# A hybrid decoder block on eight cores: the first tiles' weights by GpSimd's casting DMA, the norm weights in the row scaling, and some bf16 copies stored one tile later

## The chip, the cores and the metric

The kernel runs on all eight cores of one Trainium2 chip. Each core computes one element of the batch (8192 rows of 1024) and nothing is exchanged between cores. The metric is device time in microseconds of the slowest core.

## The reference, cut to what matters

```python
h   = rms_norm(x, norm1_g)               # y * g, y = x * rsqrt(mean(x*x) + eps)
cols = h @ w_in                          # 4864 columns: q f i g | q k v | gate_a gate_b
o_a = hgrn2_branch(...)                  # gated linear recurrence
o_b = swa_sink_attention(...)            # sliding window 128, 8 heads on 2
mixed = sigmoid(gate_a) * (o_a @ w_branch_a) + sigmoid(gate_b) * (o_b @ w_branch_b)
x   = x + mixed @ w_out
h2  = rms_norm(x, norm2_g)
x   = x + conv_glu(h2, w_up, conv_w, conv_b, w_down)   # width 2816, conv of 3 on the gate half
```

All inputs are float32. The norm weight `g` multiplies the columns of `h`, which are the rows of `w_in` (and of `w_up`), so it can be put into either factor.

## The kernel before

A core works through 16 tiles of 512 rows. For each tile `stage_a` (here A(0) to A(15)) computes everything up to `x + mixed @ w_out` and stores that as `x1scr`; `stage_f` (F(0) to F(15)) reads it back and computes the gated MLP. Inside a tile four blocks of 128 rows are normalised by `norm_block` (sum of squares on ScalarE, a power on GpSimd, the row scaling on VectorE into `xs`, transposes on TensorE, copies into `hT` or `h2T`).

The weights are cut into 61 pieces of 128 x 2048: 27 of kind A (numbers 0 to 26: f, q, aq, akv, i, g, eight gab, four wab, four wo) and 34 of kind F (22 up, 12 dn, four of the dn only 128 x 1536). They don't fit in SBUF, so every tile loads every piece again. `load_piece` does this. In tiles 1 to 15 it is one DMA on SyncE's queue, bf16, from the scratch tensor `wscr` into one of five slots `wA` or five slots `wF`. In tile 0 the source is the float32 tensor `wall`: two DMAs bring the halves of a piece into staging buffers (five in the memory of `act` for kind A, four `stg` for kind F), VectorE and ScalarE in turn multiply 128 x 256 blocks by the norm weight into the slot (or copy, for the unscaled wab, wo and dn), and the slot is then stored to `wscr`.

The order of the work on each engine is written by a planner (`schedule`): it simulates all operations with costs (`DMA_GBPS` 280, 450 ns for an issue on SyncE) and puts each engine's operations into a queue in the order of their simulated start. The chip keeps that order; every operation waits on semaphores for what it depends on. Priorities let F(i) run beside A(i+1). The chains `alA` and `alF` keep the pieces in order.

Of the kernel before, what the change touches and what calls it, by code (L numbers as in the profile page):

```python
# [9 lines left out]
F32 = mybir.dt.float32  # L10
BF16 = mybir.dt.bfloat16
# [4 lines left out]
D = 1024  # L16
# [12 lines left out]
CAPS = dict(pA=6, pF=5)  # L29
TUNE = dict(rF=1, skew=4, gc=0, foff=0.2, hold=6000.0)  # L30

# [11 lines left out]
class Pool:  # L43
    def __init__(self, name, aps):
        self.name = name
        self.aps = aps
        self.free = [(0.0, i) for i in range(len(aps))]
        self.last = [[] for _ in aps]
        self.sem = [None] * len(aps)
        self.used = {}  # L50

# [89 lines left out]
class Prog:  # L141
# [177 lines left out]
    def finalize(self):  # L319
        for e in ENGS:  # L320
            for o in self.q[e]:
                if o.dsem is not None:
                    s = o.dsem
                    if isinstance(s, VBuf):
                        if s.pool.sem[s.slot] is None:
                            s.pool.sem[s.slot] = self.new_sem()
                        s = s.pool.sem[s.slot]
                        o.dsem = s
        for o in sorted((o for o in self.ops if o.dsem is not None), key=lambda o: (o.start, o.idx)):
            self.sem_counts[o.dsem] += 16  # L330
            o.dval = self.sem_counts[o.dsem]
        for e in ENGS:
            for o in self.q[e]:
                for p in o.deps:
                    if p.dsem is None and self.needs(p, o):
                        p.signals = True
        for e in ENGS:
            c = 0
            for o in self.q[e]:
                if o.signals:  # L340
                    c += 1
                    o.sigval = c
# [158 lines left out]
def build_program(seq=SEQ):  # L501
    ntile = seq // T
    nc = bass.Bass("TRN2", target_bir_lowering=False, dynamic_dma_scratch_size=1024)
    dt_in = lambda name, shape, dt=F32: nc.dram_tensor(name, list(shape), dt, kind="ExternalInput").ap()
# [5 lines left out]
    cb_d = dt_in("cb", [128, CBN], BF16)  # L510
    c_mask = dt_in("c_mask_st", [128, 128])
    c_dm = dt_in("c_dm", [128, 2, 2, 4, 128], BF16)
    y_d = nc.dram_tensor("y", [seq, D], F32, kind="ExternalOutput").ap()
# [4 lines left out]
    with ExitStack() as es:  # L518
# [14 lines left out]
        mask_st = sb("mask_st", [128, 128], F32)  # L533
        dm = sb("dm", [128, 2, 2, 512], BF16)

# [38 lines left out]

        pWA = mkpool("wA", 5, [2048], BF16)
        pWF = mkpool("wF", 5, [2048], BF16)
        pST = mkpool("stg", 4, [1024], F32)
        pXT = mkpool("xt", 4, [D], F32)
        pX1 = mkpool("x1", 4, [D], F32)
        pSA = P.pool("sa", [act[:, 4 * i_:4 * i_ + 4, :].rearrange("p a n -> p (a n)").bitcast(F32) for i_ in range(5)])  # L580
        pXS = mkpool("xs", 2, [D], BF16)
        pFA = mkpool("fa", 8, [T], F32)
# [80 lines left out]
        def DMA(out, in_, reads, writes, sem, nbytes, eng="sp", slow=False, chain=None):  # L663
            def fn(h):
                if slow:
                    return h.dma_start(out=res(out), in_=res(in_), allow_slow_non_contiguous=True)
                return h.dma_start(out=res(out), in_=res(in_))  # L667
            return P.record(eng, fn, reads, writes, 450.0 if eng == "sp" else 100.0, 2000.0, SET_ANY, sem, nbytes, chain)

# [25 lines left out]
        cload("cf", cft[:], cf_d, 126976)  # L695
        cload("cbb", cbt[:], cb_d, 294912)
        cload("mask", mask_st[:], c_mask, 65536)
        cload("dm", dm[:], c_dm.rearrange("p a b g t -> p a b (g t)"), 524288)
# [48 lines left out]
        pidx = {(p["kind"], p["name"]): i for i, p in enumerate(pieces)}  # L747
        first_f = {}
        last_ld = {}
        bx1 = {}  # L750
# [3 lines left out]
        def load_piece(ti, kind, name):  # L754
# [6 lines left out]
            size = nk * cols  # L761
            if ti > 0:
                P.link("al" + kind, DMA(w[:, 0:size], wscr[i, :, 0:size], [bwscr[i]], [w], w, size * 256))
                return w
            hs = size // 2
            for hv in range(2):
                st = vb(pSA if kind == "A" else pST, f"st{name}{hv}")
                o_ = DMA(st[:, 0:hs], wall[i, :, hv * hs:(hv + 1) * hs], [], [st], st, hs * 512, chain="ld" + kind)
                first_f.setdefault(kind, o_)
                last_ld[kind] = o_  # L770
                if kind == "F" and first_f["F"] is o_:
                    after(o_, last_ld["A"])
                nh = nk // 2
                if p["scale"] is None:
                    eng = "dve" if hv == 0 else "act"
                    o_ = CP(eng, w[:, hv * hs:(hv + 1) * hs], st[:, 0:hs], [st], [w], n=hs, rate=2.0)
                    if hv == 0:
                        P.link("al" + kind, o_)
                else:
                    g = g1 if p["scale"] == "g1" else g2  # L780
                    koff = name[1] * 4 if name[0] == "i" else 0
                    for kk in range(nh):
                        kc = hv * nh + kk
                        o_ap, i_ap = w[:, kc * cols:(kc + 1) * cols], st[:, kk * cols:(kk + 1) * cols]
                        sc = g[:, koff + kc:koff + kc + 1]
                        if kk % 2 == 0:
                            o_ = TS("dve", o_ap, i_ap, sc, None, ALU.mult, None, [st] + C("cf"), [w], n=cols, rate=1.5)
                            if kc == 0:
                                P.link("al" + kind, o_)
                        else:  # L790
                            A(o_ap, i_ap, AF.Copy, [st] + C("cf"), [w], n=cols, scale=sc, nap=1)
                if kind == "A":
                    for o2 in st.users:
                        for c_ in range(NFC):
                            bact[c_].r.append(o2)
            if ntile > 1:
                DMA(wscr[i, :, 0:size], w[:, 0:size], [w], [bwscr[i]], P.new_sem() if False else w, size * 256)
# [5 lines left out]
        def norm_block(which, b, xv, hdst, bhdst, pool):  # L803
# [18 lines left out]
        def stage_a(ti):  # L822
# [285 lines left out]
def _in_maps(inputs, seq, n_cores):  # L1108
# [23 lines left out]
    shared["c_mask_st"] = consts["mask_st"]  # L1132
    shared["c_dm"] = consts["dm"]
    maps = []
    for c in range(n_cores):
# [12 lines left out]
```

How the kernel before makes its waits and increments, by code:

```python
    def emit(self, eng, h, ws, esems, dsems):  # L396
        for o in self.q[eng]:
            for key, val in ws[o]:
                h.wait_ge(esems[key[1]] if key[0] == "e" else dsems[key[1]], val)
            inst = o.fn(h)
            if o.dsem is not None:
                inst.then_inc(dsems[o.dsem], 16)
            elif o.signals:
                inst.then_inc(esems[eng], 1)
```

## Time and profile before

| | |
|---|---|
| times of three runs | 3827.41, 4324.09, 3821.53 us; median 3827.41 |
| profiled execution | 3824.09 us, its span 3822.6 us |
| spans of the eight cores | 3808.2 to 3822.6 us |
| granted TensorE clock, mean | 0.984 to 0.988 |
| busy | TensorE 95%, ScalarE 58%, VectorE 53%, GpSimd 12% |
| moved by the DMA engines | 772.82 MB, mean 202 GB/s |

The profile is of the slowest core. "Busy" is time in which an engine had an instruction in work. A window row gives, for one stretch, the busy time of each engine with its number of instructions, the granted TensorE clock as a share of full speed, the mean busy share of the core's 16 DMA engines and what they moved.

### The profile page before, as it was taken

To read this page: it belongs to the slowest core of one execution; us is meant where nothing else is said; L and a number is where in the kernel's file an instruction comes from. 1 tells how busy PE (TensorE), PEld (TensorE's weight loads), DVE (VectorE), ACT (ScalarE), POOL (GpSimd) and SP (SyncE) were. 2 spreads that over 40 slices of the span, in tenths; PEclk is the share of its full clock that TensorE was granted. 3 is DMA by queue.
4 is the path that set the end of the run, shared out by engine and by line. 5 is a ranking of instruction groups with operands and counts; after the bars stand their busy time and mean duration, and the time that the engine had idled before them with its cause. 6 is when DMAs were issued, how large, how long until landed. Compare 5 with 4: busy or idle time off the path is not lost.

```text
span 3822.6 us, 65864 instructions; the slowest of 8 cores (3808.2 to 3822.6 us)
## 1 busy us (share of the span) xinstructions
PE 3648.7 (95%) x21516; PEld 1969.4 (52%) x21516; DVE 2041.4 (53%) x3455; ACT 2204.0 (58%) x3771; POOL 448.0 (12%) x1082
## 2 busy tenths in 40 slices
PE   5778989999999999999999999999999999999989
PEld 2334454645546464554645546464554646455455
DVE  4546645455564546556464555645556464555634
ACT  6859566374664737467473755737466472746622
POOL 0100101101020110101011010110102011010100
PEclk8889999999999999999999999999999999999999
DMA  8798975646557465664746556474655746566454
GB/s 252 225 293 237 270 255 168 230 159 233 187 174 234 160 211 181 207 207 161 248 155 212 182 191 227 156 237 150 233 185 179 237 158 213 173 214 200 149 201 147
DMA packets 214317, 772.82 MB, mean 202 GB/s; under 512 B 23776, under 2 KB 24160, under 8 KB 213984
## 3 DMA queue, kind: packets, MB, share of 16 engines
q1 hardware_dynamic: 213408, 767.65, 60.5%
q8 instruction: 182, 2.98, 0.3%
q14 instruction: 151, 1.24, 0.1%
q10 hardware_dynamic: 576, 0.95, 0.1%
HBM read 669.94 MB, written 98.57 MB: 201 GB/s over the span
## 4 chain that ended last, share of the span: by engine, by line
PE 85%; ACT 6%; DMA 4%; issue 3%; DVE 1%; SPq 1%; POOL 0%; ACTq 0%; DVEq 0%; POOLq 0%
PE bank L651 85%; DMA wF<-wscr 3%; ACT fa L607 2%; DMA stg<-wall 1%; ACT ef L607 1%; ACT L607 1%; DMA wA<-wscr 1%; SPq L667 1%; ACT ba L607 0%; DVE fa L629 0%; ACT wF L607 0%; ACT wA L607 0%; PE bank L659 0%; ACT hT L607 0%; ACT xs L608 0%
## 5 line engine op out<-in xcount | busy, mean ns | idle before, releaser
L651 PE MATMUL bank<-h2T,wF 128*128 128x512 bf16 x5632 | 1290.5, 380 | 41.2 <-ACT ef L607 25.3
L651 PE MATMUL bank<-hT,wA 128*128 128x512 bf16 x4224 | 997.0, 387 | 48.5 <-ACT wA L607 21.3
L651 PEld LDWEIGHTS bank<-h2T,wF 128*128 128x128 bf16 x5632 | 536.5, 98 | 703.9 <-issue 97.2
L651 PEld LDWEIGHTS bank<-hT,wA 128*128 128x128 bf16 x4224 | 413.4, 99 | 527.9 <-issue 91.4
L624 DVE SCALAR_TENSOR_TENSOR ef<-bank,cft,ef 128x512 f32<-128x512 f32 x704 | 520.1, 747 | 281.9 <-ACT ef L607 236.6
L651 PE MATMUL bank<-wF,act 128*128 128x256 bf16 x5632 | 653.3, 273 | 8.7 <-DMA wF<-wscr 8.7
L651 PEld LDWEIGHTS bank<-wF,act 128*128 128x128 bf16 x5632 | 546.8, 98 | 109.4 <-issue 11.0
L607 ACT ACTIVATE ef<-bank,cft 128x512 f32<-128x512 f32 x352 | 273.2, 776 | 430.1 <-PE bank L651 383.0
L629 DVE TENSOR_TENSOR act<-ef,bank 128x512 bf16<-128x512 f32 x352 | 241.3, 686 | 406.5 <-PE bank L651 402.1
L607 ACT ACTIVATE hT<-bank 128x512 bf16<-128x512 f32 x128 | 74.3, 595 | 437.6 <-PE bank L651 436.9
L607 ACT ACTIVATE fa<-fa 128x512 f32<-128x512 f32 x400 | 239.4, 629 | 111.4 <-DVE gsum L629 105.0
L607 ACT ACTIVATE ef<-ef 128x512 f32<-128x512 f32 x352 | 213.9, 626 | 153.3 <-DVE ef L624 151.4
L607 ACT ACT_TABLE_LOAD x231 | 296.4, 1283 | 10.2 <-DVE og L619 6.1
L629 DVE TENSOR_TENSOR x<-bank,x 128x256 f32<-128x256 f32 x256 | 107.0, 422 | 284.0 <-PE bank L651 283.9
L651 PE MATMUL bank<-wA,mixT 128*128 128x512 bf16 x1024 | 234.6, 381 | 1.4 <-POOL mixT L629 1.4
L607 ACT ACTIVATE fa<-bank,sinkexp 64x128 f32<-64x128 f32 x512 | 185.3, 362 | 51.7 <-PE bank L651 24.1
L629 POOL TENSOR_TENSOR nst<-nst,mhalf 128x1 f32<-128x1 f32 x128 | 71.3, 558 | 1209.5 <-DVE nst L619 1207.4
L629 DVE TENSOR_TENSOR fa<-bank,dm 128x512 f32<-128x512 f32 x254 | 165.5, 683 | 33.8 <-PE bank L651 33.1
L607 ACT ACTIVATE ba<-fa,negshift 128x512 bf16<-128x512 f32 x254 | 171.2, 713 | 3.8 <-DVE fa L629 1.8
L624 DVE SCALAR_TENSOR_TENSOR xt<-bank,xt 128x512 f32<-128x512 f32 x128 | 88.0, 690 | 159.1 <-PE bank L651 151.2
L635 POOL COPY halo<-ef 128x2 f32<-128x2 f32 x352 | 73.8, 210 | 806.7 <-DVE ef L624 806.0
L629 POOL TENSOR_TENSOR mixT<-mixT,gbuf 128x512 bf16<-128x512 bf16 x128 | 149.5, 1169 | 136.3 <-DVE gbuf L624 135.9
(93 smaller groups left out, 3419.3 us busy)
## 6 DMA issues: line engine op xcount, KB each, us to landing
wF<-wscr SPq DMA_DIRECT2D x450, 512.0 KB, 4.5
wA<-wscr SPq DMA_DIRECT2D x405, 512.0 KB, 4.6
xt<-x SPq DMA_DIRECT2D x128, 512.0 KB, 6.1
x1scr<-xt SPq DMA_DIRECT2D x64, 512.0 KB, 4.1
xt<-x1scr SPq DMA_DIRECT2D x64, 512.0 KB, 6.9
x<-x1scr SPq DMA_DIRECT2D x64, 512.0 KB, 9.8
y<-x SPq DMA_DIRECT2D x64, 512.0 KB, 5.5
stg<-wall SPq DMA_DIRECT2D x60, 512.0 KB, 11.1
```

The costliest lines, as they stand in the source:

```text
L607: return h.activation(out=res(out), in_=res(in_), func=func, scale=scale, bias=bias)
L624: return P.record("dve", lambda h: h.scalar_tensor_tensor(out=res(out), in0=res(in0), scalar=scalar, in1=res(in1), op0=op0, op1=op1), read ...
L629: return P.record(eng, lambda h: h.tensor_tensor(out=res(out), in0=res(in0), in1=res(in1), op=op), reads, writes, cost)
L635: return P.record(eng, lambda h: h.tensor_copy(out=res(out), in_=res(in_)), reads, writes, cost)
L651: inst = h.matmul(res(out), lhsT=res(lhsT), rhs=res(rhs), start=st, stop=sp_)
L667: return h.dma_start(out=res(out), in_=res(in_))
```

## The change

In `load_piece`, a piece's first load is one DMA from `wall` (float32) issued by GpSimd, which casts to bf16 on the way straight into the slot. No staging buffers and no multiplications by VectorE or ScalarE are left. The norm weights come as a constant `c_g`, repeated over 128 partitions, and are loaded into `gB0` and `gB1`; `norm_block`'s row scaling is a scalar_tensor_tensor that multiplies by the row's factor and by `gB`. A list `keep_at` says in which tile a piece's bf16 copy is stored to `wscr`: tile 0 for pieces 0 to 17 of kind A and 0 to 9 of kind F, tile 1 for the last 9 of kind A (one gab, four wab, four wo) and the last 24 of kind F (12 up, 12 dn). These 33 pieces are loaded from `wall` by GpSimd in tile 0 and once more in tile 1. The slots of `xs` go from two to four, and a slot has a semaphore of its own for GpSimd's loads. The planner is told 1000 ns for an issue on GpSimd.

```diff
-TUNE = dict(rF=1, skew=4, gc=0, foff=0.2, hold=6000.0)
+TUNE = dict(nxt=4, nxs=4, nwa=5, nwf=5, dA=18, dF=10, dF2=99, rF=1, skew=4, gc=0, foff=0.2, hold=6000.0)
...
-    nc = bass.Bass("TRN2", target_bir_lowering=False, dynamic_dma_scratch_size=1024)
+    nc = bass.Bass("TRN2", target_bir_lowering=False, dynamic_dma_scratch_size=4096)
...
-        pST = mkpool("stg", 4, [1024], F32)
...
-        pSA = P.pool("sa", [act[:, 4 * i_:4 * i_ + 4, :].rearrange("p a n -> p (a n)").bitcast(F32) for i_ in range(5)])
-        pXS = mkpool("xs", 2, [D], BF16)
+        pXS = mkpool("xs", int(TUNE["nxs"]), [D], BF16)
...
+        cload("gB0", gB[0][:], c_g[0], 524288)
+        cload("gB1", gB[1][:], c_g[1], 524288)
...
+        keep_at = [(1 if i >= TUNE["dA"] else 0) if p["kind"] == "A" else (2 if i - na >= TUNE["dF2"] else 1 if i - na >= TUNE["dF"] else 0) for i, p in enumerate(pieces)]
...
-            if ti > 0:
+            at = keep_at[i]
+            if ti > at:
                 P.link("al" + kind, DMA(w[:, 0:size], wscr[i, :, 0:size], [bwscr[i]], [w], w, size * 256))
                 return w
-            hs = size // 2
-            for hv in range(2):
-                st = vb(pSA if kind == "A" else pST, f"st{name}{hv}")
-                o_ = DMA(st[:, 0:hs], wall[i, :, hv * hs:(hv + 1) * hs], [], [st], st, hs * 512, chain="ld" + kind)
...
+            o_ = DMA(w[:, 0:size], wall[i, :, 0:size], [], [w], w, size * 512, eng="pool")
+            P.link("al" + kind, o_)
+            last_ld[kind] = o_
+            if kind not in first_f:
+                first_f[kind] = o_
+                if kind == "F":
                     after(o_, last_ld["A"])
...
-                    for kk in range(nh):
-                        kc = hv * nh + kk
-                        o_ap, i_ap = w[:, kc * cols:(kc + 1) * cols], st[:, kk * cols:(kk + 1) * cols]
-                        sc = g[:, koff + kc:koff + kc + 1]
-                        if kk % 2 == 0:
-                            o_ = TS("dve", o_ap, i_ap, sc, None, ALU.mult, None, [st] + C("cf"), [w], n=cols, rate=1.5)
-                            if kc == 0:
-                                P.link("al" + kind, o_)
-                        else:
-                            A(o_ap, i_ap, AF.Copy, [st] + C("cf"), [w], n=cols, scale=sc, nap=1)
...
-            if ntile > 1:
+            if ti == at and ntile > at + 1:
                 DMA(wscr[i, :, 0:size], w[:, 0:size], [w], [bwscr[i]], P.new_sem() if False else w, size * 256)
             return w
...
-            TS("dve", xs.lz(), xv.lz(), st4[:, b, 2:3], None, ALU.mult, None, [xv, bn], [xs], n=D, rate=1.6)
+            STT(xs.lz(), xv.lz(), st4[:, b, 2:3], gB[which][:], ALU.mult, ALU.mult, [xv, bn] + C(f"gB{which}"), [xs], n=D, psum=False)
...
-                after(o_, P.chain["ldA" if ti == 0 else "alA"])
+                after(o_, P.chain["alA"])
```

## Rows read from the trace of the kernel before

**Rows 1.** The page: the span, and TensorE and its clock in 40 slices of 95.6 us
```profile
span 3822.6 us, 65864 instructions; the slowest of 8 cores (3808.2 to 3822.6 us)
...
PE   5778989999999999999999999999999999999989
...
PEclk8889999999999999999999999999999999999999
```

**Rows 2.** Timeline of SyncE's queue: start, us, the issues of y stores
```profile
561.79 1.27 SPq L667 DMA_DIRECT2D y<-x  x1
...
758.77 0.59 SPq L667 DMA_DIRECT2D y<-x  x1
...
984.95 0.40 SPq L667 DMA_DIRECT2D y<-x  x1
...
1211.66 0.62 SPq L667 DMA_DIRECT2D y<-x  x1
...
3478.68 0.72 SPq L667 DMA_DIRECT2D y<-x  x1
```

**Rows 3.** Windows: length, PE, PEld, DVE, ACT, POOL, PEclk, DMA share, GB/s
```profile
0.00:206.00 206.00, 137.31 (x637) 61.11 (x637) 103.46 (x215) 142.16 (x259) 23.80 (x39) 0.86 0.80 244
206.00:449.00 243.00, 200.77 (x993) 89.95 (x993) 146.06 (x279) 176.08 (x316) 27.46 (x67) 0.94 0.85 260
449.00:562.00 113.00, 97.91 (x679) 62.81 (x680) 46.66 (x88) 67.14 (x109) 4.54 (x8) 0.95 0.82 262
562.00:759.00 197.00, 188.81 (x1111) 102.88 (x1109) 105.00 (x171) 97.62 (x159) 24.82 (x61) 1.00 0.61 202
...
985.00:1212.00 227.00, 224.87 (x1347) 122.42 (x1346) 123.32 (x205) 131.49 (x225) 27.78 (x67) 1.00 0.59 196
```

**Rows 4.** Windows of 20 us, the same columns; nine had a DMA share from 0.98
```profile
140.00:160.00 20.00, 11.58 (x47) 4.58 (x45) 3.62 (x8) 17.40 (x31) 0.00 (x0) 0.74 1.00 329
...
480.00:500.00 20.00, 12.26 (x89) 6.93 (x88) 11.95 (x24) 15.05 (x27) 2.12 (x4) 0.83 0.98 296
```

**Rows 5.** The DMA view: moved in 0 to 206, 206 to 562, 562 to 759 us
```profile
DMA packets 14082, 50.26 MB, mean 244 GB/s; under 512 B 1556, under 2 KB 1940, under 8 KB 14067
...
DMA packets 25851, 92.78 MB, mean 261 GB/s; under 512 B 2876, under 2 KB 2876, under 8 KB 25821
...
DMA packets 11026, 39.80 MB, mean 202 GB/s; under 512 B 1216, under 2 KB 1216, under 8 KB 11011
```

**Rows 6.** The DMA view's issues: count, KB each, median us to landing
```profile
act<-wall SPq DMA_DIRECT2D x54, 512.0 KB, 7.2
wscr<-wA SPq DMA_DIRECT2D x27, 512.0 KB, 5.5
...
wscr<-wF SPq DMA_DIRECT2D x30, 512.0 KB, 7.5
...
wscr<-wF SPq DMA_DIRECT2D x4, 384.0 KB, 7.6
```

**Rows 7.** Groups by form, 0 to 450 us: busy us, mean ns, idle before
```profile
L607 ACT ACTIVATE wF<-stg,cft 128x256 bf16<-128x256 f32 x88 | 42.3, 502 | 37.1 <-DVE wF L619 27.7 <-DVE gsum L629 6.6 <-DVE nst L619 2.5
...
L607 ACT ACTIVATE wA<-act,cft 128x256 bf16<-128x256 f32 x68 | 32.7, 505 | 11.0 <-DVE wA L619 8.1 <-DVE gsum L629 2.7
...
L619 DVE TENSOR_SCALAR wF<-stg,cft 128x256 bf16<-128x256 f32 x88 | 31.6, 372 | 27.6 <-ACT wF L607 19.8 <-DMA stg<-wall 6.5 <-ACT fa L607 0.3
...
L624 DVE SCALAR_TENSOR_TENSOR qs<-qs,fa 128x512 bf16<-128x512 bf16 x8 | 5.1, 685 | 0.0
```

**Rows 8.** The page's costliest groups: two two-input forms of VectorE
```profile
L629 DVE TENSOR_TENSOR act<-ef,bank 128x512 bf16<-128x512 f32 x352 | 241.3, 686 | 406.5 <-PE bank L651 402.1
...
L629 DVE TENSOR_TENSOR x<-bank,x 128x256 f32<-128x256 f32 x256 | 107.0, 422 | 284.0 <-PE bank L651 283.9
```

**Rows 9.** Waits of SyncE's queue, 0 to 206 and 206 to 562 us
```profile
SPq L399 <- ACT wA L607: 113.9, 32, 14.0
...
SPq L399 <- ACT wF L607: 93.7, 37, 7.0
SPq L399 <- PE bank L651: 86.5, 22, 10.8
```

**Rows 10.** Waits of TensorE, 0 to 206 us
```profile
PE bank L651 <- ACT wA L607: 23.0, 9, 6.7
PE bank L651 <- DVE xs L619: 18.2, 4, 10.6
```

**Rows 11.** Waits of TensorE, 985 to 3400 us
```profile
PE bank L651 <- ACT ef L607: 12.8, 21, 0.9
```

**Rows 12.** The tiles xs and halo, 985 to 1212 and 206 to 562 us
```profile
L619 DVE TENSOR_SCALAR xs<-xt,nst x8: 745/750/755, 990.3 to 1179.1; 128x1024 bf16<-128x1024 f32 x8
...
L635 POOL COPY ef<-halo x22: 186/187/191, 285.4 to 446.1; 128x2 f32<-128x2 f32 x22
```

**Rows 13.** The chain that ended last, in order of time: its first long piece
```profile
23.82 12.87 PE bank L651 x48
```

More of the change, by code:

```diff
@@ L49, in __init__ @@
         self.sem = [None] * len(aps)
+        self.sem_sw = [None] * len(aps)
         self.used = {}
@@ L324, in finalize @@
                     if isinstance(s, VBuf):
[L325 to L328, printed above, removed]
+                        sems = s.pool.sem_sw if o.eng == "pool" else s.pool.sem
+                        if sems[s.slot] is None:
+                            sems[s.slot] = self.new_sem()
+                        o.dsem = sems[s.slot]
         for o in sorted((o for o in self.ops if o.dsem is not None), key=lambda o: (o.start, o.idx)):
@@ L511, in build_program @@
     c_mask = dt_in("c_mask_st", [128, 128])
+    c_g = dt_in("c_g", [2, 128, D])
     c_dm = dt_in("c_dm", [128, 2, 2, 4, 128], BF16)
@@ L533, in build_program @@
         mask_st = sb("mask_st", [128, 128], F32)
+        gB = [sb(f"gB{i}", [128, D], F32) for i in range(2)]
         dm = sb("dm", [128, 2, 2, 512], BF16)
@@ L573, in build_program @@
         act = sb("act", [128, NFC, T], BF16)
-        pWA = mkpool("wA", 5, [2048], BF16)
-        pWF = mkpool("wF", 5, [2048], BF16)
-        pST = mkpool("stg", 4, [1024], F32)
-        pXT = mkpool("xt", 4, [D], F32)
+        pWA = mkpool("wA", int(TUNE["nwa"]), [2048], BF16)
+        pWF = mkpool("wF", int(TUNE["nwf"]), [2048], BF16)
+        pXT = mkpool("xt", int(TUNE["nxt"]), [D], F32)
         pX1 = mkpool("x1", 4, [D], F32)
-        pSA = P.pool("sa", [act[:, 4 * i_:4 * i_ + 4, :].rearrange("p a n -> p (a n)").bitcast(F32) for i_ in range(5)])
-        pXS = mkpool("xs", 2, [D], BF16)
+        pXS = mkpool("xs", int(TUNE["nxs"]), [D], BF16)
         pFA = mkpool("fa", 8, [T], F32)
@@ L667, in fn @@
                 return h.dma_start(out=res(out), in_=res(in_))
-            return P.record(eng, fn, reads, writes, 450.0 if eng == "sp" else 100.0, 2000.0, SET_ANY, sem, nbytes, chain)
+            return P.record(eng, fn, reads, writes, 450.0 if eng == "sp" else (1000.0 if eng == "pool" else 100.0), 2000.0, SET_ANY, sem, nbytes, chain)
         P.stream = ("I", 0)
@@ L748, in build_program @@
         first_f = {}
+        na = sum(1 for p in pieces if p["kind"] == "A")
+        keep_at = [(1 if i >= TUNE["dA"] else 0) if p["kind"] == "A" else (2 if i - na >= TUNE["dF2"] else 1 if i - na >= TUNE["dF"] else 0) for i, p in enumerate(pieces)]
         last_ld = {}
@@ L761, in load_piece @@
             size = nk * cols
-            if ti > 0:
+            at = keep_at[i]
+            if ti > at:
                 P.link("al" + kind, DMA(w[:, 0:size], wscr[i, :, 0:size], [bwscr[i]], [w], w, size * 256))
                 return w
-            hs = size // 2
-            for hv in range(2):
-                st = vb(pSA if kind == "A" else pST, f"st{name}{hv}")
-                o_ = DMA(st[:, 0:hs], wall[i, :, hv * hs:(hv + 1) * hs], [], [st], st, hs * 512, chain="ld" + kind)
-                first_f.setdefault(kind, o_)
-                last_ld[kind] = o_
-                if kind == "F" and first_f["F"] is o_:
-                    after(o_, last_ld["A"])
[L773 to L777, printed above, removed]
-                        P.link("al" + kind, o_)
-                else:
-                    g = g1 if p["scale"] == "g1" else g2
-                    koff = name[1] * 4 if name[0] == "i" else 0
-                    for kk in range(nh):
-                        kc = hv * nh + kk
-                        o_ap, i_ap = w[:, kc * cols:(kc + 1) * cols], st[:, kk * cols:(kk + 1) * cols]
-                        sc = g[:, koff + kc:koff + kc + 1]
-                        if kk % 2 == 0:
-                            o_ = TS("dve", o_ap, i_ap, sc, None, ALU.mult, None, [st] + C("cf"), [w], n=cols, rate=1.5)
-                            if kc == 0:
-                                P.link("al" + kind, o_)
-                        else:
-                            A(o_ap, i_ap, AF.Copy, [st] + C("cf"), [w], n=cols, scale=sc, nap=1)
[L792 to L795, printed above, removed]
@@ L1133, in _in_maps @@
     shared["c_dm"] = consts["dm"]
+    shared["c_g"] = np.stack([np.tile(f("norm1_g")[0], (128, 1)), np.tile(f("norm2_g")[0], (128, 1))])
     maps = []
```

## The prediction

> **What bounds the kernel now.** I read the page first: TensorE is busy in nine tenths and more of nearly every slice, but the first five slices are the exception, and only there is the granted clock below nine tenths [rows 1]. So I looked for where the steady state begins. The issues of the last y store of each tile give it: tile 1 at 758.8 us, tile 2 at 985.0, tile 3 at 1211.7, tile 13 at 3478.7. That is (3478.7 - 985.0) / 11 = 226.7 us a tile, and tiles 1 to 2 take 226.2 already [rows 2]. Sixteen tiles at that pace are 3627 us; the span is 3822.6. The 195 us over it lie almost wholly before 759 us. In a steady tile TensorE is busy 224.9 of 227 us with 1347 matmuls, and VectorE and ScalarE stand at 123 and 131 us [rows 3]; nothing in the change makes TensorE's work less, so the steady part stays as it is.
>
> The start in three stretches [rows 3]: I, A(0), 0 to 206 us, 637 matmuls, DMA share 0.80; II, F(0) with A(1) and the beginning of A(2), 206 to 562 us, 993 + 679 = 1672 matmuls, share 0.85 and 0.82; III, F(1) with the rest, 562 to 759 us, 1111 matmuls, share 0.61. At the steady pace (226.7 us for 1347 matmuls) their work is 107, 281 and 187 us, together 576. So I loses 99 us, II loses 75, III 10. What fills I and II is DMA: 50.3 and 92.8 MB [rows 5]. In the nine windows of 20 us where the engines were full (share from 0.98) they moved 288 to 340 GB/s, mean 310 [rows 4]. At 310 the two stretches would need 162 and 299 us, against 206 and 356. The rest is idle DMA: SyncE's queue stood 114 us in I behind conversions on ScalarE and 94 us in II, since a load waits until its staging buffer has been converted, and 86.5 us behind TensorE [rows 9]. TensorE itself waited 23 us in I for ScalarE's conversions [rows 10]. Two limits lie close together, then: bytes, and the staging chain.
>
> **The change part by part.** *The conversions* go. Only the 128x256 forms cost ScalarE 32.7 + 42.3 us and VectorE 31.6 us for the F half [rows 7]; they lay in the loaded stretches (ScalarE was busy 142 of 206 us in I). This by itself is worth no time beyond the staging waits: when they are gone, the bytes are late next.
>
> *The bytes.* A stored copy is 512 KB, 0.524 MB (four of them 0.393) [rows 6]. In tile 0, 9 stores of kind A go (4.7 MB) and 24 of kind F (20 x 0.524 + 4 x 0.393 = 12.1 MB). In tile 1 these 33 pieces are read as float32 instead of bf16, which adds their bf16 size once, and stored, which adds it once more: 9.4 MB for kind A in II, 24.1 MB for kind F in III. `gB0` and `gB1` add 2 x 0.524 = 1.05 MB in I. The casting load still reads 1.049 MB a piece, as the two staged halves did. So: I 50.3 - 4.7 + 1.05 = 46.6 MB; II 92.8 - 12.1 + 9.4 = 90.1; III 39.8 + 24.1 = 63.9; sum 200.6 against 182.8 before. The change moves more in all, and moves it out of the stretches that were full into III, where the share was 0.61.
>
> *The rate.* What a casting load does to the 16 engines no row shows. Bounds: as little as its written half (0.524 MB a piece, so about 48 MB less of the 200.6), or dearer than a plain load, which a lower rate says (below). I take the plain rate by bytes read, since the nearest rows, the plain loads of the same float32 source [rows 6], were paid by what they read. How full the engines get: before, 0.80 to 0.85; at best 1. Without staging, loads wait only for slots that TensorE frees; I take 0.93 x 310 = 288 GB/s. Then the end of III comes at 5 us (start) + 200.6 / 0.288 = 702 us, against 759: 57 us earlier. By stretch it is 167, 313 and 222 us; each is above its TensorE work (107, 281, 187), so bytes still decide, in II only by a tenth. Ends: the full 310 gives 5 + 647 = 652 (107 us gained); the old fill (0.80, 0.83, 0.83 x 310) gives 188 + 350 + 248 = 786, a loss of 27 us.
>
> The Trainium skill ("DMA: Bandwidth & Descriptors", section Bandwidth) gives 6.15 us for 1 MB on the GpSimd path alone and says that transfers from 1 MiB up reach three quarters of the peak; one piece is just that size, and two or more are in flight, so it would leave my sum as it is.
>
> *GpSimd's queue.* 61 + 33 = 94 loads are issued by GpSimd. The price of such an issue is in no row; SyncE's issues take about 0.4 to 1.3 us of queue [rows 2]. At 1 us each it is 94 us on an engine that was busy 24 of 206 us in I and 32 of 356 in II [rows 3]; hidden as busy time. Not hidden of itself is the wait: a load waits for TensorE to free its slot, and behind it in the same queue stand the power of the norms, the product into `gs`, the sum into `mixT` and the two halo copies for each up piece (0.19 us each [rows 12]), for which VectorE's conv steps and then TensorE's second matmul group wait. Bounds: nothing, if the plan's order fits; 57 us and more if not (a rival, below). I take nothing, as the plan puts a load where TensorE frees the slot in its own clock, and these others need TensorE's results of about the same moment.
>
> *The row scaling.* A scaling of 1024 elements took 750 ns [rows 12]. The scalar_tensor_tensor of 512 elements with both inputs in SBUF took 685 [rows 7]; in two other two-input forms 256 more elements cost 686 - 422 = 264 ns [rows 8], so 1024 elements are 685 + 528, about 1.2 us (an estimate from these rows). That is 0.45 us more, 128 times, 58 us of VectorE, 3.6 us in each tile of 227 in which it is busy 123. TensorE's longest wait group in the steady part is 12.8 us over ten tiles, on another step [rows 11], so it has cover, and I cost it at nothing; wholly uncovered it would be 58 us. In I it stands at the head of the chain (TensorE waited 18.2 us for `xs` [rows 10]) and needs `gB0` besides: 1 to 3 us, inside the 5 us.
>
> *More `xs` slots, the semaphores, `xr` behind `alA`*: one answer, nothing.
>
> So the profiled 3824.1 us (span 3822.6 and 1.5 around it) would become 3767; the median of the runs lies 3.3 above, so 3770.
>
> **The rivals.** (a) *TensorE becomes the bound.* If a casting load costs by what it writes, the bytes are 152 MB, 528 us at 288 GB/s, below the 576 us of TensorE's work. Then the end of III is at 24 us (the first long run of matmuls begins at 23.8 [rows 13]) + 576 + 4% for waits, 623 us; 136 us gained, 3691. For it: the write side is halved. Against: the HBM side isn't.
>
> (b) *The waits move to GpSimd's queue.* SyncE waited 86.5 us in 22 waits, 3.9 us each, for TensorE to free slots [rows 9]. These now stand before halo copies and sums. If a third of the 94 loads holds TensorE for 1.8 us, the 57 us are gone: 3827. For it: one queue in order, and the real rate differs from the planned 280. Against: GpSimd is idle nine tenths of the time.
>
> The Trainium skill ("SBUF — State Buffer", the warning that VectorE blocks DMA) speaks against this change: descriptors for a GpSimd DMA can't be written while VectorE is in one of its two-port modes. No row of before shows such a DMA. As a mechanism of this kernel it would be a part of (b): each of 94 issues held by at most one VectorE scaling of 0.75 us [rows 12] is 70 us of later issues, on the path only where no slot is in reserve, and the new row scaling has two SBUF inputs and so takes the old one out of question; it gives a time within (b)'s, up to 3840, with 3 of (b)'s chances in 100.
>
> (c) *The casting load is slow*, and the kernel slower than before. The 94 loads read 96.5 MB, the rest is 104 MB, 361 us at 288. The point at which nothing is gained is (754 - 361) = 393 us for the 96.5 MB, 245 GB/s. Below it the kernel loses: at two thirds of 310, 207 GB/s, the end of III is 5 + 466 + 361 = 832, 73 us later, 3900; at half, 155 GB/s, 989, so 4057. For it: the cast is work that plain loads don't have, and 33 pieces pay it twice. Against: no row.
>
> **How the numbers follow.** The forecast, 3770, has 0.46; its own range is 3725 to 3805. (a) 0.17, (b) 0.22, (c) 0.15. A measurement of this kernel can tell 2%, 77 us: below 3751 is faster, above 3904 slower. Faster: (a) and a third of the forecast's own spread, 0.17 + 0.15 = 0.32. Slower: the part of (c) below about 205 GB/s and a remnant of (b), 0.11. Within: 0.57. For 8 in 10 the range goes from 3690, where (a) lies, to 3875, which holds (b) and the mild end of (c); left out are some 0.12 above and 0.06 below.
>
> **What would show it.** The last y store of tile 1 near 702 us and steps of 226.7 us after it; if steps are longer, the row scaling has no cover. 46.6, 90.1 and 63.9 MB in the three stretches. No ScalarE or VectorE group into `wA` or `wF`; a scalar_tensor_tensor into `xs` of about 1.2 us. In the DMA view, casting loads whose windows at full share move about 310 GB/s; (c) shows as full share at a low rate, (a) as a share that falls while TensorE is full. (b) shows as TensorE or VectorE waiting for GpSimd, and GpSimd's queue for TensorE. A higher granted clock in the first five slices goes with every gain. What would make the prediction wrong most easily is the price of the cast, which stands in no row.

## The result and the profile after

The changed kernel takes 0.9834 of the time of the kernel before, with a 95% interval of 0.9806 to 0.9863, so 3764 us where the kernel before takes 3827. That is inside 2%. (The median of its first four runs, 4025.52 us, is no measure of it: two of them ran with one or both dies at a lower clock, 4289 and 4379 us, the two others took 3760.1 and 3762.0.) Beside other experiments, on another chip, the same kernel came to 0.9829 (0.9813 to 0.9845). The prediction was 3770 us, a gain of 57; measured are 64.

The page of the changed kernel: the span, TensorE and its clock in 40 slices (of 94 us here), and the DMA queues with packets, MB and their share of the 16 engines' span. They answer to [rows 1]; the clock of the first and of the third slice is one step higher than before.

```profile
span 3758.6 us, 64664 instructions; the slowest of 8 cores (3747.6 to 3758.6 us)
...
PE   5779999999999999999999999999999999999999
...
PEclk9899999999999999999999999999999999999999
...
q1 hardware_dynamic: 191088, 687.95, 54.3%
q0 software_dynamic: 13536, 48.24, 8.2%
```

The changed kernel's timeline of SyncE's queue: the last y stores of tiles 0, 1, 2, 3 and 13, in the columns of [rows 2].

```profile
461.01 1.04 SPq L668 DMA_DIRECT2D y<-x  x1
...
716.77 1.19 SPq L668 DMA_DIRECT2D y<-x  x1
...
926.63 0.66 SPq L668 DMA_DIRECT2D y<-x  x1
...
1155.22 0.66 SPq L668 DMA_DIRECT2D y<-x  x1
...
3426.05 0.48 SPq L668 DMA_DIRECT2D y<-x  x1
```

Tile 0 is done 100.8 us earlier than in [rows 2], tile 1 only 42.0, tile 2 58.3, and tile 13 52.6. The pace from tile 2 to tile 13 is (3426.05 - 926.63) / 11 = 227.2 us, half a microsecond a tile slower than before; the last tiles gain some 11 us again, so that the spans differ by 64.0.

A tile's last y store is a poor mark in the first tiles: the planner may put more or less of the next tile's work before it. A better one is how far TensorE has come. It does 21516 weight loads (PEld) in every kernel here; before, 637 of them were done at the end of stretch I, 2310 at the end of II and 3419 at the end of III [rows 3]. The same amounts of work in the changed kernel:

```profile
0.00:185.00 185.00, 126.31 (x626) 59.52 (x638) 77.05 (x133) 101.68 (x178) 39.89 (x71) 0.91 0.83 183
185.00:502.00 317.00, 288.06 (x1644) 152.04 (x1673) 171.51 (x275) 184.65 (x306) 52.37 (x119) 0.97 0.89 225
502.00:697.00 195.00, 185.91 (x1089) 101.30 (x1107) 109.03 (x174) 121.11 (x200) 38.69 (x79) 0.99 0.90 223
```

The table has the times in us, from a core's first instruction, at which these loads and three others begin, the median of the eight cores. "Order" is the number of the 21516 places at which TensorE's weight loads, in the order of the trace, have other tiles than in the changed kernel (buffer numbers left out).

| kernel | order | 637 | 1976 | 2310 | 3419 | 5000 | last |
|---|---|---|---|---|---|---|---|
| before | 5850 | 206 | 512 | 563 | 758 | 1026 | 3812 |
| changed | 0 | 184 | 448 | 501 | 695 | 964 | 3750 |
| changed, beside experiments 5, 10 and 11 | 0 | 184 | 447 | 500 | 693 | 963 | 3750 |
| 1, nothing put off | 2248 | 184 | 462 | 511 | 705 | 974 | 3759 |
| 2, half the read bytes | 1836 | 182 | 434 | 488 | 675 | 945 | 3732 |
| 9, eight operations that hold a slot | 2272 | 194 | 469 | 526 | 729 | 999 | 3786 |
| 10, eight free operations | 1930 | 190 | 459 | 515 | 719 | 988 | 3774 |
| 11, four free operations | 1954 | 187 | 452 | 506 | 707 | 985 | 3772 |
| 12, 14 pieces of kind F put off | 1787 | 184 | 478 | 529 | 727 | 997 | 3783 |
| 13, six slots | 1989 | 189 | 462 | 514 | 714 | 990 | 3786 |

So I takes 184 us in the place of 206, II 317 in the place of 356, III 194 in the place of 196. The gain is made in I and II, 22 and 39 us, and III costs nothing although the put-off stores lie there.

Windows of the changed kernel, in the columns and stretches of [rows 3]:

```profile
0.00:206.00 206.00, 138.03 (x676) 64.48 (x689) 86.43 (x150) 112.03 (x193) 39.89 (x71) 0.90 0.85 193
206.00:449.00 243.00, 225.47 (x1267) 117.83 (x1287) 136.10 (x218) 144.17 (x239) 48.18 (x105) 0.98 0.91 213
449.00:562.00 113.00, 108.50 (x628) 56.15 (x638) 60.24 (x91) 81.09 (x135) 14.23 (x43) 1.00 0.74 212
562.00:759.00 197.00, 187.69 (x1133) 105.60 (x1152) 104.39 (x168) 112.17 (x186) 34.47 (x66) 0.99 0.90 243
...
985.00:1212.00 227.00, 222.35 (x1317) 122.26 (x1338) 126.92 (x203) 130.45 (x223) 29.65 (x67) 1.00 0.57 194
```

(Some matmul records are missing from this trace, so the weight loads, PEld, are the better count.) In 206 to 449 us TensorE did 1287 instead of 993 at a clock of 0.98 instead of 0.94, while ScalarE was busy 144 instead of 176 us. In 562 to 759 us the DMA share rose from 0.61 to 0.90, since the stores that were put off lie there, and TensorE still did 1152 weight loads where it did 1109 before.

The DMA view of the changed kernel by tile ends, 0 to 187 us (the x1 store of A(0)), 187 to 461 and 461 to 717 us: everything moved, and of it GpSimd's queue. They answer to [rows 5].

```profile
DMA packets 9717, 34.37 MB, mean 184 GB/s; under 512 B 1068, under 2 KB 1452, under 8 KB 9706
...
q0 software_dynamic: 4234, 15.44, 52.8%
...
DMA packets 16957, 61.42 MB, mean 224 GB/s; under 512 B 1883, under 2 KB 1883, under 8 KB 16934
...
q0 software_dynamic: 5846, 20.74, 47.0%
...
DMA packets 16245, 58.33 MB, mean 228 GB/s; under 512 B 1800, under 2 KB 1800, under 8 KB 16223
...
q0 software_dynamic: 3456, 12.06, 31.5%
```

A casting load is counted here by what it writes. Counted by what it reads, the three stretches moved 34.37 + 15.44 = 49.8, 82.2 and 70.4 MB, at 266, 300 and 275 GB/s; together 202.4 MB by 717 us.

The tile xs in 985 to 1212 us of the changed kernel, against [rows 12]: 1.28 us in the place of 0.75.

```profile
L625 DVE SCALAR_TENSOR_TENSOR xs<-xt,nst,gB x8: 1274/1280/1286, 1055.2 to 1123.6; 128x1024 bf16<-128x1024 f32 x8
```

Waits in the first 760 us of the changed kernel, GpSimd's and TensorE's longest:

```profile
POOL nst L630 <- DVE nst L620: 163.8, 19, 56.8
POOL wF L668 <- PE bank L652: 124.4, 35, 16.3
POOL halo L636 <- DVE ef L625: 112.0, 39, 11.0
POOL wA L668 <- PE bank L652: 65.4, 18, 11.3
```
```profile
PE bank L652 <- DVE xs L625: 32.6, 8, 20.2
PE bank L652 <- ACT ba L608: 12.6, 5, 5.5
PE bank L652 <- DMA wA<-wscr: 8.4, 1, 8.4
PE bank L652 <- DVE nst L620: 6.0, 2, 4.7
PE bank L652 <- POOL mixT L630: 5.2, 2, 3.3
```

GpSimd stands 190 us waiting for TensorE to free slots, and yet TensorE waits for GpSimd hardly at all (5.2 us for `mixT`, and 3.3 for `gs`). TensorE's longest wait, 20.2 us, is the first `xs`.

### The profile page after: what moved, and what is told of

Its sections match the earlier page's. It is cut to its first block, busy times and chain, and to the rows that moved or that the text cites. A ratio compares the mean times of both kernels' runs of the same rounds, so it can differ in the third digit from the quotient of the medians.

```text
span 3758.6 us, 64664 instructions; the slowest of 8 cores (3747.6 to 3758.6 us)
## 1 busy us (share of the span) xinstructions
PE 3604.0 (96%) x21154; PEld 1968.3 (52%) x21516; DVE 2046.0 (54%) x3275; ACT 2128.2 (57%) x3595; POOL 520.6 (14%) x1176
## 3 DMA queue, kind: packets, MB, share of 16 engines
q0 software_dynamic: 13536, 48.24, 8.2%
## 4 chain that ended last, share of the span: by engine, by line
PE 86%; ACT 6%; issue 3%; DMA 3%; DVE 1%; POOL 0%; ACTq 0%; another core or an unknown queue 0%; DVEq 0%; SPq 0%; POOLq 0%
PE bank L652 86%; ACT fa L608 2%; DMA wF<-wscr 1%; ACT ef L608 1%; ACT L608 1%; ACT xs L609 1%; DMA wA<-wscr 1%; DMA gB<-c_g 0%; ACT ba L608 0%; DVE fa L630 0%; DMA wF<-wall 0%; DVE ef L625 0%; DMA wA<-wall 0%; PE bank L660 0%; ACT hT L608 0%
## 5 line engine op out<-in xcount | busy, mean ns | idle before, releaser
L652 PE MATMUL bank<-hT,wA 128*128 128x512 bf16 x4069 | 963.1, 381 | 24.8 <-DMA wA<-wscr 8.4
L609 ACT ACTIVATE xs<-xt 128x1024 bf16<-128x1024 f32 x128 | 134.6, 1053 | 225.9 <-DMA xt<-x1scr 225.7
L636 POOL COPY halo<-ef 128x2 f32<-128x2 f32 x352 | 83.6, 238 | 1276.8 <-DVE ef L625 1276.5
L630 DVE TENSOR_TENSOR x<-bank,x 128x256 f32<-128x256 f32 x256 | 105.7, 422 | 228.0 <-PE bank L652 227.5
L608 ACT ACTIVATE fa<-bank 128x512 f32<-128x512 f32 x192 | 106.6, 596 | 178.6 <-PE bank L652 132.1
L625 DVE SCALAR_TENSOR_TENSOR xs<-xt,nst,gB 128x1024 bf16<-128x1024 f32 x128 | 164.2, 1292 | 52.3 <-POOL nst L630 43.4
```

The costliest lines, as they stand in the source:

```text
L608: return h.activation(out=res(out), in_=res(in_), func=func, scale=scale, bias=bias)
L609: return h.activation(out=res(out), in_=res(in_), func=func, scale=scale, bias=bias, accum_out=accum)
L625: return P.record("dve", lambda h: h.scalar_tensor_tensor(out=res(out), in0=res(in0), scalar=scalar, in1=res(in1), op0=op0, op1=op1), read ...
L630: return P.record(eng, lambda h: h.tensor_tensor(out=res(out), in0=res(in0), in1=res(in1), op=op), reads, writes, cost)
L636: return P.record(eng, lambda h: h.tensor_copy(out=res(out), in_=res(in_)), reads, writes, cost)
L652: inst = h.matmul(res(out), lhsT=res(lhsT), rhs=res(rhs), start=st, stop=sp_)
```

## The experiments

Each was timed against the kernel before on its own chip; the ratios are to that, with 95% intervals. Differences between two experiments are differences of ratios, times 3827 us. One thing weakens nearly all of them: the planner sees the edit and writes another order for all engines. The table above says how far TensorE's order moved. Only experiments 7 and 8 leave it nearly as it was (5 and 6 places), and experiment 13, which adds one buffer and no work, comes out 42 us slower with its new order.

**1. Nothing put off.** All bf16 copies are stored in tile 0.

```diff
-TUNE = dict(..., dA=18, dF=10, dF2=99, ...)
+TUNE = dict(..., dA=99, dF=99, dF2=99, ...)
```

> The changed kernel with every bf16 copy stored in tile 0, as in the kernel before. 16.8 MB less are moved in tiles 0 and 1 together. Theory (bytes decide where they are over TensorE's work): stretch I has 51.3 MB, 178 us; II 92.8 MB, 322 us; III 39.8 MB, below TensorE's 187 us; end of III near 692 us, so some 10 us faster than the changed kernel, about 3750. Rival (putting the stores off is what gives the gain): 20 to 40 us slower than the changed kernel, 3780 to 3800.

Measured: 0.9868 (0.9847 to 0.9889), 51 us faster than before and 13 slower than the changed kernel. Its last y stores of tiles 0 to 2, from the timeline of SyncE's queue (the first line holds three stores, the last of them at 498.6), and the window in which it does the work of III:

```profile
497.34 1.67 SPq L668 DMA_DIRECT2D y<-x  x3
...
714.19 0.59 SPq L668 DMA_DIRECT2D y<-x  x1
...
940.18 0.61 SPq L668 DMA_DIRECT2D y<-x  x1
```
```profile
513.00:708.00 195.00, 186.26 (x1074) 101.33 (x1073) 106.36 (x168) 106.85 (x175) 28.25 (x64) 0.98 0.56 188
```

This kernel moves nearly as many bytes as the kernel before, and has most of the gain. It is neither 10 us faster, as the theory had it, nor 20 to 40 slower, as the rival did; its interval overlaps that of the changed kernel's first measurement (to 0.9863), not of the second (to 0.9845). Tile 0 is done 38 us later than in the changed kernel, tile 1 2.6 us earlier and tile 2 13.5 later, which most likely is the planner's order at work. By weight loads it is level at the end of I and some 10 us behind at the end of II, and stays so. The work of III takes it 195 us at a DMA share of 0.56, and the changed kernel 195 us at 0.90: the bytes put off into III cost nothing there.

**2. Half the read bytes.** GpSimd's first loads read random bf16 numbers; the real weights are left out.

```diff
-            o_ = DMA(w[:, 0:size], wall[i, :, 0:size], [], [w], w, size * 512, eng="pool")
+            o_ = DMA(w[:, 0:size], wbf[i, :, 0:size], [], [w], w, size * 256, eng="pool")
```

> The changed kernel, but GpSimd's first loads read a bf16 tensor of random numbers of the same shape and don't cast (the real weights are left out): same bytes written, half read. Theory (a casting load costs the DMA engines what it reads): 48 MB less, the start becomes bound by TensorE, 50 to 70 us faster than the changed kernel, 3690 to 3710. Rival (it costs what it writes, or the start is bound by TensorE already): the same as the changed kernel within 10 us, 3760.

Measured: 0.979 (0.9774 to 0.9805), 17 us faster than the changed kernel. GpSimd's queue on its page, and the windows in which it does the work of I and of III:

```profile
q0 software_dynamic: 13024, 48.24, 4.2%
```
```profile
0.00:183.00 183.00, 125.29 (x638) 57.90 (x639) 77.34 (x133) 98.92 (x176) 38.74 (x71) 0.93 0.60 195
...
489.00:677.00 188.00, 183.16 (x1101) 101.86 (x1099) 105.89 (x167) 111.44 (x182) 39.70 (x81) 0.99 0.76 249
```

Two things are read here. The price of the cast: the same 48.24 MB written took 4.2% of 3746.7 us of the 16 engines plain, 157 us, and 8.2% of 3758.6, 308 us, cast. So a casting load costs what it reads: 96.5 / 308 is 313 GB/s, near the 48.24 / 157 = 307 of the plain loads and the 310 of full engines in [rows 4]. And what bytes are worth: 48 MB less in two tiles gave 17 us, not 50 to 70. The point of the forecast's theory that failed is here. The work of I takes 182 us in the place of 184, although the DMA share falls from 0.83 to 0.60; II takes 306 in the place of 317, and III 187 in the place of 194. What holds TensorE in I is not bytes, then. That it is A(0)'s own chain is likely, and no run shows it.

**3. The same from SyncE's queue.** The load of experiment 2 without `eng="pool"`.

> As the run with half the bytes read, its first loads issued by SyncE instead of GpSimd. Theory (GpSimd's queue is free enough): the same within 10 us. Rival (loads that wait in GpSimd's queue hold up halo copies, norms and sums): 15 to 40 us faster than that run.

Measured: 3742.7 us in one run, against 3744.1 to 3748.3 for experiment 2. GpSimd's queue costs nothing that can be told.

**4. Only the norm weights moved.** The kernel before with the new row scaling and plain copies in the staging. In float32 the two constants don't fit in SBUF beside the staging buffers (a last tensor needs 4104 bytes a partition, 3992 are left), so they and the causal mask are held in bf16.

```diff
-                if p["scale"] is None:
+                if True:
...
-            TS("dve", xs.lz(), xv.lz(), st4[:, b, 2:3], None, ALU.mult, None, [xv, bn], [xs], n=D, rate=1.6)
+            STT(xs.lz(), xv.lz(), st4[:, b, 2:3], gB[which][:], ALU.mult, ALU.mult, [xv, bn] + C(f"gB{which}"), [xs], n=D, psum=False)
```

> The kernel before, staging and all, with only the norm weights moved into the row scaling (they and the causal mask are held in bf16, so that all fits); the staged halves are copied plainly, one copy by VectorE and one by ScalarE a piece. Theory (the gain comes from loads that no longer wait for staging buffers): conversions cost half, but the buffers stay in the way; at most 20 us faster than before, 3805 to 3825. Rival (the conversions' engine time and their place in the two queues was the cost, not bytes): most of the gain, 3775 to 3790.

Measured: 1.0009 (0.9972 to 1.0045). By itself this part brings nothing, even though the conversions take 105 us of VectorE and ScalarE together, before 170.

**5. Plain copies alone.** Only the first line of that diff; the norm weights are left out.

> The kernel before with plain copies of the staged halves in the place of the multiplications (the norm weights are left out; old row scaling, no constants gB): half the conversions' engine time. Theory (engine time counts by itself; in the run with only the scaling moved, the dearer scaling and the constants took it back): 10 to 20 us faster than before. Rival (the staging buffers set the pace, whatever a conversion costs): within 6 us of before.

Measured: 0.9939 (0.9920 to 0.9958), 23 us faster than before. The rival, that a conversion's cost doesn't matter, falls. But engine time by itself isn't shown: a shorter conversion also frees its staging buffer earlier, and SyncE's waits behind conversions in 0 to 562 us fell from 228 us to 191. Nothing of the gain is made in A(0), where TensorE begins weight load 637 at 207 us, against 206 before; all of it is there at load 2310 (533 against 563). Set against experiment 4, on another chip and in another order (5148 places), the new scaling and its constants cost the staged kernel some 27 us.

**6. No row scaling by gB.** The changed kernel with the old scaling, without the two constants (the norm weights are left out).

> The changed kernel with the old row scaling and without the constants gB (the norm weights are left out). Theory (the dearer scaling has cover, the two constants at the start have none): 6 to 12 us faster than the changed kernel, all of it before the first long run of matmuls, with 226.7 us a tile afterwards. Rival (the scaling isn't covered in the steady part): 0.5 us a block and more, 40 to 60 us faster.

Measured: 0.9861 (0.9818 to 0.9903), no faster than the changed kernel. Neither theory gives this: the steady part has cover, as forecast (from weight load 5000 to 20000, 1344.75 loads a tile, cores 0 to 3 take 227.5 us a tile with the old scaling and 227.4 in the changed kernel, so that the half microsecond over the 226.8 of before isn't the scaling's), but what the constants cost at the start doesn't come back when they go. TensorE's order differs at 1201 places. So the 27 us between experiments 4 and 5 are not a price of the scaling that holds everywhere.

**7. Norm weights first.** `gB0` is loaded ahead of all constants, `gB1` behind them.

> The changed kernel with the first norm weights loaded ahead of all other constants and the second behind them. Theory (TensorE's 20 us wait at the start is for that load): 5 to 9 us faster than the changed kernel. Rival (the whole set of first transfers shares the engines, so that the order of the issues matters little): 0 to 3 us.

Measured: 0.9845 (0.9789 to 0.99), the same. The first line of TensorE's waits in 0 to 206 us says why:

```profile
PE bank L652 <- DMA cbt<-cb: 20.4, 1, 20.4
```

In the changed kernel it waited 20.2 us for `xs`, which waited for `gB0`; now it waits 20.4 us for the identity. The first transfers share the engines, and their order only chooses the one that is late.

**8. Fewer bytes in the first 20 us.** Norm weights in bf16; `gB1`, the mask and the attention bias are issued behind the third piece.

```diff
+            if ti == 0 and name == ("q", 0):
+                for n_ in ("gB1", "mask", "dm"):
+                    after(bconst[n_].w, o_)
```

> The changed kernel with the norm weights in bf16 (half the bytes) and with the second norm's weights, the mask and the attention bias issued behind the third weight piece. Theory (the first 20 us are one set of transfers that shares the engines, so bytes must leave it, not change places): the first long run of matmuls begins 3 to 5 us earlier and the kernel is 3 to 8 us faster than the changed one. Rival (what is gained at the start is given back, since A(0) is bound by its own chain later): no difference.

Measured: 0.9828 (0.9774 to 0.9882), not to be told from the changed kernel. From the chain that ended last, in order of time, of the changed kernel and then of this one:

```profile
1.99 16.65 DMA gB<-c_g
...
32.98 5.61 PE bank L652 x17
```
```profile
1.99 16.56 DMA gB<-c_g
...
30.01 21.16 PE bank L652 x80
```

The load of half the size takes as long, and 3 us earlier at the first long run of matmuls are not seen in the end: the rival. TensorE's order is the same but for six places, and the lead is gone inside the first tiles: 2 us at weight load 637, none at 2310 (502 against 501).

**9. Engine time that holds a slot.** Eight operations of 128x256 a piece in tile 0, four on VectorE and four on ScalarE, that wait for the piece's load.

```diff
+            if ti == 0:
+                for kk in range(8):
+                    if kk % 2 == 0:
+                        TS("dve", dmy[0][:], gB[0][:, 0:256], 1.0, None, ALU.mult, None, [w] + C("gB0"), [bdmy[0]], n=256, rate=1.5)
+                    else:
+                        A(dmy[1][:], gB[0][:, 0:256], AF.Copy, [w] + C("gB0"), [bdmy[1]], n=256, nap=1)
```

> The changed kernel, with eight idle operations of 128x256 for each piece in tile 0 added, four on VectorE and four on ScalarE, of the kinds the conversions had; each waits for the piece's load, and TensorE waits for none of them. Theory (conversions cost through what waits for them, in the staging): at most 10 us slower than the changed kernel. Rival (their engine time on ScalarE and VectorE is what cost): 30 to 60 us slower, most of the way back to the kernel before.

Measured: 0.9923 (0.9901 to 0.9946), 34 us slower than the changed kernel: the size that the rival gave. How much of it is engine time, held slots or another order isn't shown.

**10. Engine time alone.** The same without `[w]`, placed in the queues behind the issue of the load by `after(d_, o_)`.

> As the run with idle copies, but they wait for nothing and hold no slot: the same eight operations a piece stand in VectorE's and ScalarE's queues behind the issue of the piece's load. Theory (engine time is what cost, 1.5 and 2.0 us a piece): still 30 to 45 us slower than the changed kernel, 3790 to 3805. Rival (in the other run they cost by holding the slot until they were done): within 12 us of the changed kernel.

> The eight free operations a piece once more beside the changed kernel on the same chip: 25 to 40 us slower than it if engine time is what they cost; under 10 us if the first measurement was the chip's.

> The changed kernel again, on the chip of the runs beside it, as their measure: 0.983 of the kernel before.

The first time, without the changed kernel beside it, two runs took 3787.8 and 3798.9 us. Beside the changed kernel on one chip: 0.9893 (0.9874 to 0.9912) against 0.9829 (0.9813 to 0.9845), 24 us slower. What was added, in 0 to 760 us, as groups by form (busy us, mean ns):

```profile
L609 ACT ACTIVATE dmy<-gB 128x256 bf16<-128x256 f32 x244 | 101.3, 415 | 22.3 <-DMA gB<-c_g 8.0 <-ACT dmy L609 0.4
L621 DVE TENSOR_SCALAR dmy<-gB 128x256 bf16<-128x256 f32 x244 | 76.7, 314 | 18.4 <-DVE dmy L621 0.5
```

That is 178 us together; the conversions of the kernel before took 170 (the largest groups are in [rows 7]). TensorE waits for none of it, no slot is held, and the kernel is still 24 us slower. That is not yet the price of the engine time. At weight load 637 it is 6 us behind, at load 1976 12. Its last free operation begins at 448 us, before load 1976, and it falls back by another 14 us after that (988 against 963 us at load 5000), where no added operation is left; the order still differs there, and the delay may have effects of its own.

**11. Half of that.** Four operations a piece.

> The changed kernel with four free operations a piece instead of eight. If the engine time costs in proportion, half of what the eight cost, 12 to 20 us; if the engines have cover until they are nearly full, under 6 us.

Measured: 0.9883 (0.9863 to 0.9902), 21 us slower than the changed kernel. Half the engine time costs as much as all of it, within the intervals. It isn't a sum of durations, then; neither form of the expectation holds. At weight load 637, inside A(0), it does look like one: 3 us behind here, 6 there. But the last free operation begins at 442 us, it is 5 us behind at load 1976, and the other 17 us come later.

**12. Only 14 pieces of kind F put off.** `dF=20`.

> The changed kernel with only 14 instead of 24 pieces of kind F stored in tile 1. 5.2 MB go from F(1)'s stretch to F(0)'s, and as much is saved. Theory (F(1)'s stretch ran with the DMA engines full between 562 and 702 us, F(0)'s at 0.9): 5 to 10 us faster than the changed kernel. Rival (F(0) needs the room): 5 to 14 us slower, towards the run with nothing put off.

Measured: 0.9893 (0.9821 to 0.9965), probably slower than the changed kernel and surely not 10 us faster, so the theory on where there is room was wrong again. Putting off 14 pieces of kind F is no better than putting off nothing (experiment 1, 0.9868) and worse than 24. It is 30 us behind at weight load 1976, where experiment 1, with more stores before that point, is 14 behind: bytes don't explain that, and another order is the likely reason.

**13. Six slots wA.** `nwa=6`.

> The changed kernel with six slots wA instead of five. Theory (the loads in flight are enough, the engines' queues are full before 206 us): within 8 us of the changed kernel. Rival (GpSimd's load waits for a slot, 65 us for kind A, and that starves the DMA engines): 10 to 25 us faster.

Measured: 0.9944 (0.991 to 0.9977), 42 us slower. Neither theory allowed for that: one more buffer and otherwise the same kernel, but the planner writes another order (1989 places on TensorE). That is as many places as in the experiments with free operations, and more time.

## Why the prediction came out as it did, step by step

*What bounds the kernel.* Right on where the time can be won: at weight load 3419 the changed kernel is 63 us ahead, at the last one 62. The pace then went from 226.7 to 227.2 us.

*The bytes.* Right in amount: 200.6 MB forecast for the three stretches, 202.4 MB by the end of tile 1. *The rate.* 288 GB/s was assumed, 282 measured (202.4 MB in 717 us, or 284 from the forecast's start at 5 us); a casting load costs what it reads, 313 GB/s with the engines full, where 310 was assumed. Rivals (a) and (c) fall with this number: (a) needed 157 us for the casting loads and (c) over 390; they took 308.

*The sum.* 702 us were forecast for the end of III. By equal work it came at 695, and the stretches were 167, 313 and 222 us by forecast and 184, 317 and 194 by measurement: I was longer by 17 us, II by 4, III shorter by 28. The total is near because these errors cancel, which is luck.

*The step that failed* is "each is above its TensorE work (107, 281, 187), so bytes still decide", and before it "when they are gone, the bytes are late next". The term of the sum that was wrong by most is III: 63.9 MB at 288 GB/s, 222 us. It took 194 us, 7 more than TensorE's work of 187. These are the bytes of the work of III in the changed kernel:

```profile
DMA packets 12157, 43.54 MB, mean 223 GB/s; under 512 B 1343, under 2 KB 1343, under 8 KB 12139
...
q0 software_dynamic: 3456, 12.06, 41.3%
```

That is 43.54 + 12.06 = 55.6 MB by reading, 8 less than costed, at 285 GB/s. Alone it would look as if bytes had decided, and only their amount had been too high; experiment 1 speaks against that, with 195 us for the same work at a DMA share of 0.56. In I bytes didn't decide either: 184 us, and 182 with half the bytes read (experiment 2), where 167 were forecast. In II they have a part: 306 us with half the bytes read, 317 in the changed kernel. All told, 48 MB less gave 17 us in the place of 50 to 70, and 17 MB less (experiment 1) gave none and went with 13 us more.

*The conversions* were costed at nothing beyond the staging waits. Whether that is wrong stays open. Experiments 5, 9, 10 and 11 move the time by 23, 34, 24 and 21 us, but each has another order, 5 shortens the staging waits too, and of the 24 and 21 us in 10 and 11 some 14 and 17 arise after the last operation that was added. What is left to engine time as such is about 6 us in A(0) (10), 3 with half of it (11). An argument for more would be that ScalarE, busy 142 of 206 us in [rows 3], was nearly full between 100 and 160 us, where A(0)'s attention and recurrence run through it. Two of these windows from the trace of before, in the columns of [rows 4], which has the third (ScalarE 17.40, TensorE 11.58 of 20 us):

```profile
100.00:120.00 20.00, 13.39 (x89) 7.00 (x88) 13.26 (x26) 18.48 (x35) 1.15 (x1) 0.76 0.29 86
120.00:140.00 20.00, 16.99 (x64) 6.44 (x63) 11.45 (x20) 18.31 (x37) 2.30 (x2) 0.81 0.63 184
```

In both the DMA engines were far from full. But the changed kernel, which has no conversions, fills ScalarE as much while it does this work:

```profile
100.00:120.00 20.00, 16.11 (x89) 7.83 (x91) 8.39 (x14) 17.35 (x30) 2.81 (x4) 0.91 1.02 234
120.00:140.00 20.00, 14.07 (x67) 6.19 (x67) 3.91 (x6) 18.91 (x32) 3.96 (x5) 0.89 0.69 168
```

And experiment 5, with less conversion time, is no faster in A(0).

*Where the 64 us are.* By stretch: 22 us in I, 39 in II, 1 or 2 in III. By part of the change: putting stores off, 10 to 13 (experiment 1, as far as its other order costs nothing). The other 51 go with the casting load as a whole, which takes away the conversions, the staging buffers and the waits in SyncE's queue [rows 9] together; no run takes them apart.

*The moved stores* were costed as bytes that change their stretch. In II the forecast was right: 9 us for 2.7 MB less, and experiment 1 takes 327 us there, 10 more than the changed kernel. In III they were costed at 35 us over TensorE's work, and cost none. That is why experiment 1 was expected to be 10 us faster and is 13 slower.

*GpSimd's queue*, nothing: right. An issue took 0.55 us, its 94 loads 52 us; it stood 190 us before slots; 3 agrees, and with it rival (b) falls. The "DVE blocks DMA" warning of the Trainium skill ("SBUF — State Buffer", section "SBUF: two separate sides"), that GpSimd can't write a DMA's descriptors while VectorE is in a two-port mode, had the chance of a small part of (b). GpSimd's issues look like this in 0 to 760 us (groups: busy us, mean ns, idle before), and a hold by VectorE isn't visible:

```profile
L668 POOL DMA_DIRECT2D wF<-wall x58 | 31.6, 548 | 147.0 <-PE bank L652 124.4 <-DMA wscr<-wF 14.6 <-DVE ef L625 5.1
...
L668 POOL DMA_DIRECT2D wA<-wall x36 | 20.0, 558 | 67.2 <-PE bank L652 65.4 <-issue 0.8 <-DMA wscr<-wA 0.7
```

*The row scaling*, 1.2 us forecast and 1.28 measured, with cover: right in the steady part (6). *Its constants*, 1 to 3 us, were costed too low at the start: TensorE's first matmul came at 20.2 us instead of 10.6, and the first long run at 33.0 instead of 23.8 [rows 13], 9 us. Making it 3 us less brought nothing (8).

## What to carry to other kernels

Compare two versions by equal work (how many weight loads the bounding engine has done), not by the time of one store: a planner may move the store, as tile 0 shows (101 us earlier by its last store, 62 by work at the end). A DMA share of 0.90 and a rate near the full one don't show that bytes set the time: take the bytes away and see, as experiments 1 and 2 do. Where a planner writes the order, a changed parameter is a changed order: count in the traces how many instructions stand elsewhere, and look at when the difference arises, before reading 20 us as a price. Where the time of added work is lost mostly after its last operation, its duration isn't the price.

## What the runs showed that was not expected

A casting load from float32 to bf16 takes the DMA engines as long as a plain load of its source's bytes (308 us for 96.5 MB read, against 157 us for 48.24 MB of plain loads), while the profile counts its written bytes; at a full share some windows show about 200 GB/s instead of 300, which would look like a slow transfer to someone who reads the rate alone. A window of the changed kernel, in the columns of [rows 4]:

```profile
80.00:100.00 20.00, 17.20 (x105) 8.23 (x106) 12.05 (x19) 17.84 (x30) 2.76 (x4) 1.00 1.02 202
```

What stays open: what a conversion's engine time costs by itself, what holds TensorE in A(0), why six slots cost 42 us, why half of the free operations cost as much as all, and why the new scaling with its constants costs 27 us in the staged kernel and nothing in the changed one. In all the experiments that bear on these the planner wrote another order, and none was run with the order held fixed.
